# Expert layers of a transformer step: gathers that come out turned, eight places for the weights, scatter rows found once

## What is computed

```
hid = silu(xi @ w1[e]) * (xi @ w3[e])     # w1, w3: 1024 x 512
y   = hid @ w2[e]                         # w2: 512 x 1024
```

## Time and profile before

| what | us |
|---|---|
| median of 3 runs (lowest to highest) | 1731.25 (1730.42 to 1731.63) |
| the profiled execution, its own time | 1736.72 |
| its span, first to last instruction | 1734.9 |
| TensorE products busy in it (8379 of them, as many weight loads) | 1542.3 |
| DVE, ACT, POOL busy | 454.4, 301.9, 145.8 |
| instructions in all | 21413 |

### The profile page before, as it was taken

The page is one execution under the profiler, slowest core; times in us unless marked ns, Lnnn a source line. Parts: engine busy times, 40 slices in busy tenths (PEclk is TensorE's granted clock), DMA queues, the critical chain, the costliest instruction groups (busy, mean ns, idle before and its releaser), DMA issues.

```text
span 1734.9 us, 21413 instructions
## 1 busy us (share of the span) xinstructions
PE 1542.3 (89%) x8379; PEld 727.6 (42%) x8379; DVE 454.4 (26%) x1067; ACT 301.9 (17%) x614; POOL 145.8 (8%) x200
## 2 busy tenths in 40 slices
PE   6799876796999999999957997796999999999991
PEld 4355764444433333333323444544433333333330
DVE  0031375533311111111123023643311111111113
ACT  3100212412111111111111003521111111111112
POOL 1101103100000000000004000010000000000000
PEclk9899987897999999999977998897899999999995
DMA  9996944105999999999969422023599999999982
GB/s 351 241 346 215 384 145 149 52 26 206 418 428 428 429 427 428 427 428 427 429 244 304 166 97 85 1 77 133 216 424 428 429 427 427 428 429 427 428 360 112
DMA packets 82918, 521.62 MB, mean 301 GB/s; under 512 B 10130, under 2 KB 11610, under 8 KB 56240
## 3 DMA queue, kind: packets, MB, share of 16 engines
q1 hardware_dynamic: 69536, 485.58, 68.6%
q0 software_dynamic: 13328, 35.29, 6.6%
HBM read 511.08 MB, written 20.22 MB: 306 GB/s over the span
## 4 chain that ended last, share of the span: by engine, by line
PE 81%; DVE 9%; DMA 4%; ACT 2%; SPq 2%; issue 1%; POOL 0%; DVEq 0%; POOLq 0%; ACTq 0%
PE psum L840 25%; PE psum L853 13%; PE psum L528 13%; PE psum L821 10%; PE psum L786 5%; PE psum L846 3%; DMA ring<-in_ab_w_in 2%; PE psum L833 2%; SPq L364 2%; PE psum L827 2%; PE psum L452 1%; PE psum L701 1%; PE psum L714 1%; DVE area_q L1248 1%; DVE area_m L1248 1%
## 5 line engine op out<-in xcount | busy, mean ns | idle before, releaser
L840 PE MATMUL psum<-ring,area_t 128*64 128x512 f32 x1024 | 449.9, 592 | 1.8 <-issue 1.0
L841 PE MATMUL psum<-ring,area_t 128*64 128x512 f32 x1024 | 450.0, 592 | 0.0
L840 PEld LDWEIGHTS psum<-ring,area_t 128*64 128x64 f32 x1024 | 140.1, 137 | 291.9 <-issue 291.9
L853 PE MATMUL psum<-ring,area_t 128*64 128x512 f32 x1024 | 237.2, 606 | 2.2 <-DVE area_t L1751 2.2
L528 PE MATMUL psum<-ring,area_t 128*128 128x512 f32 (+1 forms) x528 | 223.0, 584 | 7.4 <-DMA ring<-in_ab_w_in 7.4
L1722 DVE COPY area_q<-psum 64x512 f32<-64x512 f32 x64 | 44.4, 694 | 567.4 <-PE psum L841 567.3
L821 PE MATMUL psum<-area_h,area_t 128*64 128x512 f32 x768 | 180.5, 606 | 3.0 <-DVE area_t L1736 3.0
L528 PEld LDWEIGHTS psum<-ring,area_t 128*128 128x128 f32 x528 | 101.6, 193 | 125.5 <-issue 116.1
L1931 POOL DMA_INDIRECT pair_rows<-area_q,idx x64 | 62.4, 974 | 933.6 <-ACT area_q L1163 919.1
L841 PEld LDWEIGHTS psum<-ring,area_t 128*64 128x64 f32 x1024 | 140.1, 137 | 0.0
L853 PEld LDWEIGHTS psum<-ring,area_t 128*64 128x64 f32 x1024 | 69.6, 138 | 124.4 <-issue 124.4
(11 more groups left out here) (251 smaller groups left out, 1365.4 us busy)
## 6 DMA issues: line engine op xcount, KB each, us to landing
ring<-in_moe_w SPq DMA_DIRECT2D x192, 2048.0 KB, 14.5
ring<-in_ada_w SPq DMA_DIRECT2D x24, 2048.0 KB, 18.8
ring<-in_na_w_in SPq DMA_DIRECT2D x6, 2048.0 KB, 17.4
ring<-in_ab_w_in SPq DMA_DIRECT2D x5, 2048.0 KB, 24.0
area_m<-mod_ready POOLq DMA_DIRECT2D x6, 1024.0 KB, 9.5
area_q<-pair_rows POOLq DMA_DIRECT2D x6, 1024.0 KB, 7.2
ring<-in_ab_w_out SPq DMA_DIRECT2D x2, 2048.0 KB, 16.0
area_g<-mod_ready POOLq DMA_DIRECT2D x4, 1024.0 KB, 8.4
```

The lines of the kernel that those rows point to most:

```text
L840: pe.matmul(banks[2 + u][0:64, :], lhsT, w1[:, k, :], start=(k == 0), stop=(k == KT - 1))
L841: mm = pe.matmul(banks[2 + u][64:128, :], lhsT, w3[:, k, :], start=(k == 0), stop=(k == KT - 1))
L853: mm = pe.matmul(banks[6 + u][64 * j:64 * j + 64, :], hidT[u][:, k, :], w2[:, k, 512 * j:512 * j + 512], start=(k == 0), stop=(k == 3))
```

## The change

**The gather.** h is now the stationary side and four experts' selections, 256 columns, the moving one: `gather` writes rows that are turned already. The four experts of a quad q are gathered in four parts g, each of a quarter of the 1024 values (two blocks k, three token tiles t), during the four experts before; each part in two halves, the first between hidden(e) and turn_hidden(e), the second behind turn_hidden(e). The first quad is made in parts of four blocks k and two experts; two of them stand ahead of expert 0, and experts 1 and 2 carry two parts. The last four experts carry none. The transposes, the one-column products and ACT's token copy go; DVE copies the turned rows (`turn`), and `pick` works on four experts at a time.

**The rows of the scatter** are found once in each layer: `rank_slots` on DVE, six products in `places` on TensorE behind expert 0's second half, one `index`.

**The ring** gets two more places in `area_mg` (`area_m` and `area_g`, now one allocation): 6 is modA and modB, 7 the rest of `area_m` with `mixed`, and modG. Chunks 6 to 71 of the experts go over eight places, always to the one whose chunk is oldest, chunks 72 to 95 over six. Chunk 6 waits for `x_mixed`, chunk 7 for `h_ready`.

**POOL's loads** of modulation vectors for after the experts move behind scatter 23, the last expert with a chunk in a new place, and wait for its `y_done`.

**No loops:** all 32 experts are written out on every engine. `weigh` moves behind expert 12 (`WEIGH_AT`). The overflow part gets its own index.

```diff
 RING = 6
+PLACES = 8
...
+EXTRA_FROM, EXTRA_TO = 6, 72
...
-        area_g = sb("area_g", [P, 2 * D])
+        area_mg = sb("area_mg", [P, 6144 + 2 * D])
+        area_m, area_g = area_mg[:, 0:6144], area_mg[:, 6144:]
...
+        sel4 = [area_t[:, 768 * i:768 * i + 768].rearrange("p (t e s) -> p t e s", t=NT, e=4) for i in range(2)]
+        xT4 = [area_q[:, 5120 + 2048 * i:7168 + 2048 * i].rearrange("p (k s) -> p k s", k=KT) for i in range(2)]
+        slots = area_q[:, 3352:4120].rearrange("p (k t s) -> p k t s", k=2, t=NT)
...
+        idx = cond32[:, 0, :].bitcast(U32)
...
+        TAKEN, LANDING, BEFORE, LAST_EXTRA = [], [], [], [0, 0]
+        _latest, _count = [-1] * PLACES, [0] * PLACES
+        for _n, (_kind, _l, _c) in enumerate(stream):
+            _extra = _kind == "moe" and EXTRA_FROM <= _c < EXTRA_TO
+            _to = min((7, 6, *range(RING)) if _extra else range(RING), key=lambda i: _latest[i])
+            TAKEN.append(_to)
+            BEFORE.append(_latest[_to])
+            _latest[_to], _count[_to] = _n, _count[_to] + 1
+            LANDING.append(_count[_to])
+            if _to >= RING:
+                LAST_EXTRA[_l] = _c // 3
...
+            return ring[:, TAKEN[n], :] if TAKEN[n] < RING else area_mg[:, CHUNK * (TAKEN[n] - RING):][:, 0:CHUNK]
...
+        GATHERS = {0: ((0, 2),), 1: ((0, 3), (1, 0)), 2: ((1, 1), (1, 2)), 3: ((1, 3),)}
+        for _e in range(4, EXPERTS - 4):
+            GATHERS[_e] = ((_e // 4 + 1, _e % 4),)
+        for _e in range(EXPERTS - 4, EXPERTS):
+            GATHERS[_e] = ()
...
-                if n >= RING:
-                    freed(sp, n - RING)
+                if BEFORE[n] >= 0:
+                    freed(sp, BEFORE[n])
...
+                for c in range(3 * EXPERTS):
+                    n = NUM["moe", l, c]
+                    if c == EXTRA_FROM:
+                        sp.wait_ge(S["x_mixed"], (l + 1) * NT * OUT_CHUNKS)
+                    if c == EXTRA_FROM + 1:
+                        sp.wait_ge(S["h_ready"], NT * (2 * l + 2))
+                    load(n, chunk(n), expert_dram(l, c // 3, c % 3))
...
-            def turn_tokens(e, u, base):
...
-                token_turns().then_inc(M["xT_done"], 1)
...
+            def gather(l, q, g, halves):
+                n = 4 * (QUADS * l + q) + g
+                if 0 in halves:
+                    pe.wait_ge(M["sel_ready"], l * PICKS + (1 + g // 2 if q == 0 else 2 + q))
+                    if n >= 2:
+                        pe.wait_ge(M["xT_copied"], n - 1)
+                if q == 0:
+                    ks, cols = range(4 * (g % 2), 4 * (g % 2) + 4), slice(2 * (g // 2), 2 * (g // 2) + 2)
+                else:
+                    ks, cols = range(2 * g, 2 * g + 2), slice(0, 4)
+                w = 64 * (cols.stop - cols.start)
+                for i, k in enumerate(ks):
+                    if 2 * i // len(ks) not in halves:
+                        continue
+                    for t in range(NT):
+                        mm = pe.matmul(banks[n % 2][:, w * i:w * i + w], h[:, t, k * P:k * P + P],
+                                       sel4[q % 2][:, t, cols, :].rearrange("p e s -> p (e s)"),
+                                       start=(t == 0), stop=(t == NT - 1))
+                if 1 in halves:
+                    mm.then_inc(M["xT_done"], 1)
...
+            def places(l):
+                pe.wait_ge(S["slots_ready"], l + 1)
+                for k in range(2):
+                    for t in range(NT):
+                        mm = pe.matmul(banks[5][:, 0:EXPERTS], slots[:, k, t, :], val[k][:, t, :],
+                                       start=(k == 0 and t == 0), stop=(k == 1 and t == NT - 1))
+                mm.then_inc(S["places_done"], 1)
...
+                    return xT4[(e // 4) % 2][:, k, 64 * (e % 4):64 * (e % 4) + 64]
...
-                one(0, 0, False)
-                one(1, 1, False)
-                with pe.Fori(1, EXPERTS // 2 - 1) as i:
-                    for u in range(2):
-                        one(pe.snap(i * 2 + u), u, False)
-                one(EXPERTS - 2, 0, False)
-                one(EXPERTS - 1, 1, True)
+                gather(l, 0, 0, (0, 1))
+                gather(l, 0, 1, (0, 1))
...
+                    hidden(l, e, *(lambda k, n=n: wchunk(n, KT)[:, k, :] for n in up))
+                    ahead = GATHERS[e]
+                    if len(ahead) == 1:
+                        gather(l, *ahead[0], (0,))
+                    elif ahead:
+                        gather(l, *ahead[0], (0, 1))
+                    turn_hidden(l, e)
+                    if len(ahead) == 1:
+                        gather(l, *ahead[0], (1,))
+                    elif ahead:
+                        gather(l, *ahead[1], (0, 1))
+                    if e == 0:
+                        places(l)
+                    n = NUM["moe", l, 3 * e + 2]
+                    pe.wait_ge(landed[place(n)], when(n))
+                    down(l, e, wchunk(n, 4))
...
-            def copy_tokens(e, base):
...
-                act.copy(tok, banks[0][:, :]).then_inc(M["tok_copied"], 1)
...
-                stt(val, o2, 2.0, last(keep[:, KEEP["pair"]], EXPERTS), ALU.mult, ALU.add)
...
+            def rank_slots(l):
+                for k, (oh, rank) in enumerate(((o1, m1), (o2, m2))):
+                    ts(pval[:, k, :], keep[:, KEEP["pair"]], 2.0 * k, None, ALU.add)
+                    tt(val[k], oh, last(pval[:, k, :], EXPERTS), ALU.mult)
+                    tt(c32, oh, key, ALU.mult)
+                    red(rank, c32, ALU.add)
+                    tt(slots[:, k, :, :], lead(keep[:, KEEP["slot"]], NT), last(rank, P), ALU.is_equal,
+                       "dve_step" if k == 0 else "slots_ready")
...
+            def turn(l, q, g):
+                n = 4 * (QUADS * l + q) + g
+                v.wait_ge(M["xT_done"], n + 1)
+                if q >= 2:
+                    v.wait_ge(M["hid_done"], l * EXPERTS + 4 * (q - 1))
+                if q == 0:
+                    dst = xT4[0][:, 4 * (g % 2):4 * (g % 2) + 4, 128 * (g // 2):128 * (g // 2) + 128]
+                    src = banks[n % 2][:, :].rearrange("p (k s) -> p k s", k=4)
+                else:
+                    dst = xT4[q % 2][:, 2 * g:2 * g + 2, :]
+                    src = banks[n % 2][:, :].rearrange("p (k s) -> p k s", k=2)
...
+            def pick(l, e0, e1):
+                q = e0 // 4
+                if q >= 2:
+                    v.wait_ge(M["xT_done"], turned(l, q - 2, 3))
+                n = e1 - e0
+                for t in range(NT):
+                    ins = v.tensor_tensor(sel4[q % 2][:, t, e0 - 4 * q:e1 - 4 * q, :],
+                                          lead(keep[:, KEEP["slot"]][:, 0:BLOCK], n), last(key[:, t, e0:e1], BLOCK),
+                                          ALU.is_equal)
+                ins.then_inc(M["sel_ready"], 1)
...
-                whole(EXPERTS - 2, 0, 1)
-                whole(EXPERTS - 1, 1, 0)
+                pick(l, 0, 2)
+                pick(l, 2, 4)
+                for g in range(2):
+                    turn(l, 0, g)
+                rank_slots(l)
+                pick(l, 4, 8)
+                for e in range(EXPERTS):
+                    one(l, e)
+                    if len(GATHERS[e]) > 1:
+                        turn(l, *GATHERS[e][0])
+                    product(l, e)
+                    if GATHERS[e]:
+                        turn(l, *GATHERS[e][-1])
+                    if e % 4 == 0 and e // 4 + 2 < QUADS:
+                        pick(l, e + 8, e + 12)
+                    if e == 0:
+                        index(l)
+                    if e == WEIGH_AT:
...
+                pool.wait_ge(S["places_ready"], l + 1)
                 for e in range(EXPERTS):
-                    scatter(M, e, e % 2, base, l)
+                    scatter(M, e, e % 2, base, l, idx[:, e:e + 1])
+                    if e == LAST_EXTRA[l]:
+                        pool.wait_ge(M["y_done"], base + e + 1)
+                        load_G(l, 1)
+                        if l == 0:
+                            load_AB(1, 0)
+                        else:
...
```

More of the change, by code:

```diff
@@ L325, in wchunk @@
         def wchunk(n, k):
-            return ring[:, place(n), :].rearrange("p (k n) -> p k n", k=k)
+            return chunk(n).rearrange("p (k n) -> p k n", k=k)
         def expert_dram(l, e, j):
-            one = (l, e) if isinstance(e, int) else (l, bass.ds(e, 1))
             k = 4 if j == 2 else KT
@@ L376, in load_experts @@
             def load_experts(l):
[L377 to L386, removed]
-                            sp.wait_ge(M["y_done"] if j == 2 else M["hid_done"], e + (l * EXPERTS - 1))
-                        sp.dma_start(dst, expert_dram(l, e, j)).then_inc(landed[at], 16)
-                one(0, 0)
-                one(1, 1)
-                with sp.Fori(1, EXPERTS // 2) as i:
-                    for u in range(2):
-                        one(sp.snap(i * 2 + u), u)
```

(23 more changed lines are left out.)

214 lines of the change are left out of this document (81 added, 133 removed).

## The result

The change made the kernel **slightly slower**, by 0.3 to 0.5%: median 1743.16 us of 20 runs against 1734.39 of 20 runs of the kernel before beside them, ratio 1.0042 (95% interval 1.0033 to 1.0051). In a second comparison it was 1740.19 against 1735.21, 1.0031 (1.0018 to 1.0043). The forecast was 1721.6, with a range up to 1733. The profiled execution took 1742.06, its span 1740.2. Of the 21.6 us between forecast and median, 3.1 lie in the starting point: the forecast started from a median of three runs, 1731.25, where 20 runs gave 1734.39. For the profiled execution the forecast was 1727.0, and 15.1 us are to be explained.

What follows compares the result with a forecast made beforehand. It took TensorE as today's bound, the DMA close behind and bounding after the change; 2.8 us off in layer 0 and 6.9 in layer 1 gave 9.7 off, 1731.25 to 1721.6 us, range 1712 to 1733.

Steps and rivals of the forecast that it cites:

- All at nothing: DVE works 60 of 370 us: Other engines in the expert stage: ACT's and DVE's changed work, including weigh at expert 12, was priced at zero.
- So the DMA becomes the bound: Expert stage: DMA's 15.0 us an expert against TensorE's 13.6; from near expert 16 TensorE waits some 1.4 us in each.
- Straight-line code: Instruction fetches for 26 more expert copies a layer: 0.26 MB, 16 fetches, 0.6 us of DMA a layer.
- The start: First gathers before expert 0: hidden products start at 421.9 instead of 421.18, cost 0.7 us, bounds 0.3 and 3.4.
- The two places: Ring, before the experts: chunks 6 and 7 load early, two chunks less remain, 10.0 us in each layer.
- POOL's loads: Behind expert 23: 1 MB loads cost their bytes, 7.4 us in layer 0 and 3.7 in layer 1.
- A: Rival, expert stage: POOL's loads cost twice their bytes, 22.2 us, so the gain is gone, 1732.7; chance 0.11.
- B: Rival, expert stage: POOL's loads cost nothing, 1710.5; chance 0.09.
- D: Rival, expert stage: TensorE stops at each of 16 fetches a layer; at 7.9 us each, 1921; chance 0.08.
- E: Rival, expert stage: the DMA is no bound and keeps up with 13.6 us an expert, 1669; chance 0.02.
- F: Rival, ring: the two extra chunks bring nothing, 20 us more, 1741.6; chance 0.03.
- C: Rival: TensorE's waits make its clock fall; what is left is a late rise at the start, 2.7 a layer, 1727; chance 0.11.

Runs made afterwards that it cites:

- pick_later: Changed kernel with DVE's comparisons for experts 8 to 11 moved from behind expert 0 to behind expert 3: median 1734.77 us, 0.9987 of the kernel before.
- spread: loads_last with the second quad gathered like the first, double gathers moved from experts 1 and 2 to 5 and 6: 1716.18 us, 0.9892 of the kernel before.
- loads_last: pick_later with POOL's loads waiting until the last expert weights have landed: 1724.44 us, 0.9928 of the kernel before.
- six_places: Changed kernel with all chunks over six places and POOL's loads before the experts as before: 1752.77 us, 1.0096 of the kernel before.
- turns_thrice: loads_last with the hidden turns of every expert made three times: 1741.29 us, 1.0045 of the kernel before.
- half_w2: pick_later with half of each w2 left unloaded, serving only for its time: 1682.64 us (one run).
- after_again: The changed kernel run again without an edit: 1740.19 us, 1.0031 of the kernel before.
- loads_last_2: loads_last once more, on another chip as the comparison for further runs: 1725.51 us, 0.9950 of the kernel before.

## Why the prediction was wrong

**Where the forecast failed: "All at nothing: DVE works 60 of 370 us".** I had priced DVE by busy time (60 of 370 us) and looked at one burst, `weigh`. I did not follow what each DVE instruction waits for and what is queued behind it: `pick(l, 8, 12)` behind expert 0 waits for a gather of expert 1, in front of expert 1's copy. Measured by pick_later: 4.2 to 4.8 us in each layer. This is the largest part of the miss, and it is shown.

**Second, "So the DMA becomes the bound", taken as continuous from the first release.** The sum let the chunks follow one another at the average pace of the kernel before, 5.01 us. A load leaves only when TensorE frees a place, and in experts 1 and 2 TensorE needs 16.4 and 16.3 us, more than the DMA's 15.0, while the queue is short. I had counted these 5.2 us on TensorE, found that TensorE had time, and dropped them. By the landings in pick_later, chunk 10 at 447.7 and chunk 19 at 495.6 are 47.9 us apart. In the kernel before, the chunks at the same place behind the first release, 8 (447.2) and 17 (493.4), are 46.2 apart: 1.8 us lost in layer 0, and by the same landings 3.1 in layer 1 (48.9 against 45.7). spread takes this loss away, and its runs show the direction and less exactly the size.

**Third, "Straight-line code", priced by its bytes at 0.6 us.** From chunk 20 to chunk 95 the landings take 374.1 and 374.9 us in the kernel before. In loads_last, spread, six_places and the repeats of the first two, where POOL's loads stay out of this stretch, they take 376.4 to 378.7, some 2.7 us more in each layer. The extra time stands at single chunks. In expert 19 above it is chunk 59, which lands at 700.2, 6.4 us behind chunk 58 at 693.7, and chunk 60 follows 5.0 us later, so the loss stays. A fetch of code stands just before that landing:

```profile
L394 SPq DMA_DIRECT2D ring<-in_moe_w x1: 328/328/328, 664.5 to 664.5; - x1
DMA to landing us min/median/max: 29.3/29.3/29.3
...
L394 SPq DMA_DIRECT2D ring<-in_moe_w x2: 328/380/432, 671.3 to 671.7; - x2
DMA to landing us min/median/max: 28.8/31.2/33.5
...
q8 instruction: 1, 0.02, 6.6%
```

The last row is the instruction queue in the window 697 to 698. In the ten profiles in which the weights bound the stage (all but before, turns_thrice and half_w2), I took the chunks from 21 on, without those beside POOL's loads: 1384 landings that the traces hold. 40 of them came over 5.5 us behind the landing before, and 38 of these 40 have a fetch of 8 or 16 KB in the 2 to 7.2 us ahead of them, a stretch chosen after looking; of all 1384 only 304 have one. The kernel before, with one or two fetches in this part of a layer for 16 to 18, has no such chunk. six_places has the late chunks too, so the new places are not their cause. That the fetches are is argued from these times; no run took them away.

The three make some 8.6 us where 8.2 are missing in layer 0 (4.4, 1.8, and 3.0 less the 0.6 forecast, by the first profile after without POOL's 7.4) and 9.4 where 9.0 are missing in layer 1 (4.2, 3.1, and 2.7 less 0.6, without POOL's 3.7). They also fit what stays in spread: against the sum without POOL's loads (446.9 and 446.5) it runs 3.5 and 3.1 us longer.

**Right, by its steps.** TensorE's expert: 13.6 forecast, 13.71 measured. Without the DMA the run was forecast at 426.1 (421.9 to 848), and half_w2 has 431.5: 5.4 more, 0.1 us for each expert and 1.8 in the three before the last, in one of which the clock fell. It ends at 850.4, close to 848, only because it started 3 us early. The DMA 15.0. The start: 0.7 late forecast, 0.9 early measured, but the key was ready 1.5 us earlier in that execution (411.72 for 413.27), so 0.6 late against it. The waits: first forecast near expert 16, found at 18. The two places: 10 us a layer; six_places, with the loads' bytes, agrees within 0.5 us in each layer (0.8 against after_again). POOL's loads, 7.4 us in layer 0: the two long experts take 18.41 and 19.06 where 30.0 would be the DMA's time for two, 7.5 more; in layer 1 six experts from the loads on take 95.3 for 90.0, 5.3 where 3.7 was forecast, with one of the chunks behind a fetch among them; the same loads cost 3.8 in the three experts from there on in pick_later (48.8 for 45.0). By the figure of the Trainium skill (DMA: Bandwidth & Descriptors, Measured), 6.15 us for each, three would be 18.5; beside a full stream of weights the trace does not agree, they cost their bytes.

**The rivals.** A and B (loads at twice or none of their bytes) are out. D, a stop of TensorE at each fetch of code, is out: the instruction queue grew from 38 to 65 packets, yet no hole but those for weights and for the copies of expert 1 and of the last four experts appears. What the fetches touch is the stream of weights, and there by far less. E, a DMA that keeps up, is out by the waits, F by six_places. C, the clock, did appear: it fell behind the holes, and where the wait behind could pay for it the end did not move, as written. Before the experts 4 to 27 of the ten profiles stand 189 waits of up to 1.9 us, none of them followed by a slow start, and 18 waits of 2.0 to 4.5 us, 13 of them followed by hidden products at the 1.2 GHz level for a while, 1.3 to 2.7 us longer (that at 788.65 was, that at 807.71 was not). The Trainium skill (TensorE: Matmul & The Clock Gate, HAM oscillation) describes a loop whose waits for a DMA are longer than its bursts and each of whose bursts starts cold; the waits of about 1.1 us here are short beside bursts of 13.7, and the trace shows no cold start behind them. None of the rivals on the slow side was the right one: that side held a wait which I had not looked for. That the range ended at 1733, near the 1734.4 of the kernel before, is not to the forecast's credit, since nothing in it stood for this wait.

Of the chances, 0.75 for faster was too much for a kernel in which the DMA's lead at the start decides, since each microsecond of delay there stays to the end. The mechanism that the forecast lived on, the two places, was there: some 10 us a layer, 9.2 us of run in the two layers together once POOL's loads have taken theirs (six_places against after), and it was not enough.

## What to carry to other kernels

When a change makes the DMA the bound, the engines' work matters only by when it gives back buffers: follow each release in the first few rounds, where the queue is shortest, and give the double work to later rounds. Before a step is moved in the queue of an idle engine, write down what it waits for and who is queued behind it; a busy share of 16% hid the costliest wait of this change. Transfers that are not needed soon belong behind the last load of a stage that the DMA bounds, and written-out code is to be counted among the transfers, by what these times suggest.

## What was not expected of the hardware

The DMA's pace in the bound part is so even (14.97 to 15.05 us in most experts) that TensorE's starts are a ruler, and the periods of 15.2 to 16.6 us between them point at single chunks that came late or at a fall of the clock. That a fetch of 16 KB may go with a delay of up to 1.8 us for a chunk of 2 MB, and another one with none, I had not expected; its bytes alone are 0.04 us of the full queue. In the stretch between the stages the time differed by some us from profile to profile with the same code: in the attention of layer 1 the profile before stood 27 us at half clock and the one after 38 us (2 (1 - granted clock), summed over windows of 2 us), loads_last 27 and loads_last_2 again 38. The whole stretch took 347.7 us before and 349.9 after, but 346.2 in loads_last and 351.3 in loads_last_2: one profile of each kernel would have put its 2.2 us on the change.
